# Up projections of three feed-forward blocks by seven half products in place of eight

## The reference

```
# first block, D_FF = 4096
z = rms_norm(h, norm_mlp_g);   h = h + square(relu(z @ w_up)) @ w_down
...                            # gated ple layer, final norm
# second block, D_FF_2 = 2816
def swiglu(x, w_in, w_out):
    gate, up = jnp.split(x @ w_in, 2, axis=-1)
    return (jax.nn.silu(gate) * up) @ w_out
h = h + 0.5 * rms_norm(swiglu(rms_norm(h, ffn1_pre_g), ffn1_w_in, ffn1_w_out), ffn1_post_g)
...                            # mixer: dilated attention and a state-space part (S5)
h = h + 0.5 * rms_norm(swiglu(rms_norm(h, ffn2_pre_g), ffn2_w_in, ffn2_w_out), ffn2_post_g)
```

## Time and profile before

| | |
|---|---|
| time, median of 3 runs | 3018.67 us (3018.64 to 3019.09) |
| span of the profiled execution | 3016.7 us, 2.0 below the median of the runs; no other time of it is given |
| TensorE busy | 2998.1 us, 99% |
| VectorE, ScalarE, GpSimd busy | 1351.8, 870.4, 408.9 us |
| moved by DMA | 206.98 MB, mean 69 GB/s |

### The profile page before, as it was taken

One profiled execution on the slowest core, in us unless ns is written; L12 is line 12 of the kernel. 1 busy time (PEld: TensorE's weight loads), 2 busy tenths in 40 slices (PEclk: granted clock), 3 DMA queues, 4 the chain that ended last, 5 costly groups with the idle time before them and its releaser, 6 DMA issues.

```text
span 3016.7 us, 36793 instructions
## 1 busy us (share of the span) xinstructions
PE 2998.1 (99%) x14144; PEld 2465.9 (82%) x14144; DVE 1351.8 (45%) x1735; ACT 870.4 (29%) x1328; POOL 408.9 (14%) x1004
## 2 busy tenths in 40 slices
PE   8999999999999999999999999999999999999999
PEld 7788888888888888888888888887788888888887
DVE  5854444444445453333333353346655333333335
ACT  6524122112214352111111143136744111111112
POOL 0010000000000001988860010012100000000000
PEclk9999999999999999999999999999999999999999
DMA  3131111111112121222221132212131111111113
GB/s 131 41 108 53 56 56 49 35 56 56 42 42 68 45 85 49 75 97 100 89 82 42 49 133 84 78 63 98 55 133 70 49 49 49 58 54 42 42 49 133
DMA packets 54553, 206.98 MB, mean 69 GB/s; under 512 B 7232, under 2 KB 8000, under 8 KB 52144
## 3 DMA queue, kind: packets, MB, share of 16 engines
q1 hardware_dynamic: 38736, 140.53, 13.9%
q0 software_dynamic: 15712, 65.02, 5.9%
HBM read 173.15 MB, written 31.20 MB: 68 GB/s over the span
## 4 chain that ended last, share of the span: by engine, by line
PE 97%; DVE 2%; ACT 1%; issue 0%; DMA 0%; SPq 0%; DVEq 0%; ACTq 0%
PE ps L128 30%; PE ps L130 30%; PE ps L129 30%; PE ps L1976 1%; PE ps L268 1%; PE ps L1991 1%; PE ps L1950 1%; PE ps L340 0%; PE ps L1626 0%; DVE acc L179 0%; ACT junk L200 0%; PE ps L1659 0%; DVE acc L187 0%; PE ps L1667 0%; ACT junk L166 0%; PE ps L1639 0%
## 5 line engine op out<-in xcount | busy, mean ns | idle before, releaser
L128 PE MATMUL ps<-region_a,region_b 128*128 128x512 f32 x1664 | 654.9, 394 | 1.0 <-DVE region_a L227 1.0
L130 PE MATMUL ps<-region_a,region_b 128*128 128x512 f32 x1664 | 648.0, 389 | 0.0
L129 PE MATMUL ps<-region_a,region_b 128*128 128x512 f32 x1664 | 647.5, 389 | 0.0
L128 PE MATMUL ps<-region_b,region_a 128*128 128x512 f32 x1088 | 428.2, 394 | 0.1
L130 PE MATMUL ps<-region_b,region_a 128*128 128x512 f32 x1088 | 424.9, 391 | 0.0
L947 DVE TENSOR_TENSOR acc<-acc,ps 128x1024 f32<-128x1024 f32 x240 | 292.9, 1220 | 294.0 <-PE ps L130 294.0
L129 PE MATMUL ps<-region_b,region_a 128*128 128x512 f32 x1088 | 424.5, 390 | 0.0
L123 DVE TENSOR_TENSOR region_b<-raw,region_b 128x1024 fp32r<-128x1024 f32 x176 | 216.2, 1244 | 348.5 <-ACT region_b L119 348.2
L128 PEld LDWEIGHTS ps<-region_a,region_b 128*128 128x128 f32 x1664 | 312.5, 188 | 66.4 <-issue 1.8
L130 PEld LDWEIGHTS ps<-region_a,region_b 128*128 128x128 f32 x1664 | 312.4, 188 | 65.2
L129 PEld LDWEIGHTS ps<-region_a,region_b 128*128 128x128 f32 x1664 | 312.6, 188 | 64.3 <-issue 1.7
(11 more groups left out here) (302 smaller groups left out, 3233.6 us busy)
## 6 DMA issues: line engine op xcount, KB each, us to landing
raw<-stream SPq DMA_DIRECT2D x252, 512.0 KB, 3.3
ssm_row<-ssm_mid POOLq DMA_DIRECT2D x8, 1632.0 KB, 7.3
x_mid<-acc POOLq DMA_DIRECT2D x24, 512.0 KB, 3.1
ssm_mid<-made_osc POOLq DMA_DIRECT2D x8, 1024.0 KB, 4.3
ssm_mid<-made_out POOLq DMA_DIRECT2D x8, 608.0 KB, 3.4
acc<-x SPq DMA_DIRECT2D x8, 512.0 KB, 8.1
rold<-x POOLq DMA_DIRECT2D x16, 256.0 KB, 3.7
old_a<-x_mid POOLq DMA_DIRECT2D x8, 512.0 KB, 8.2
```

Source lines behind the costliest of these rows:

```text
L128: nc.tensor.matmul(psum, lhs(0), rhs(0), start=first, stop=False)
L129: nc.tensor.matmul(psum, lhs(0), rhs(1), start=False, stop=False)
L130: return nc.tensor.matmul(psum, lhs(1), rhs(0), start=False, stop=last)
```

## The change

An up pair is now two weight units (256 channels: for `mlp` two hidden blocks, for the gated feeds a gate and an up block). The product of a 2 x 2 arrangement of weight halves (inputs 0 to 511 and 512 to 1023, by column block) with a 2 x 2 arrangement of token pieces (the same input halves, near and far tokens) is formed from seven half products with sums made first (Strassen's scheme in the form with 4 sums of weights and 4 of tokens) and seven joins of results. All up products of a feed come first; the hidden units go to DRAM (`hid`), and are read back for the down products, which run for the near tokens and then for the far ones, each tile summed in PSUM over all hidden units.

The core of the diff:

```diff
-CHUNK = 2
+        SLOTS_UP, AHEAD, AHEAD_DOWN = 7, 6, 3
+        NEAR_K, FAR_K = 2, 4
+        class Quick:
+                order = [(0, 1), (0, 2), (1, 1), (1, 2), (0, 5), (1, 5), (0, 6), (1, 6), (0, 7), (1, 7), (0, 4), (0, 3),
+                         (2, 1), (1, 4), (2, 2), (1, 3)]
+                for p in range(2, pairs):
+                    order += [(p, 6), (p, 7), (p, 4), (p, 5)] + ([(p + 1, 1), (p + 1, 2)] if p + 1 < pairs else []) + [(p, 3)]
...
+            def ring_at(self, i):
+                return (0, 1, 2, 3, 0, 1, 2, 3, 2, 3, 2, 3, 0, 2, 3, 0)[i] if i < 16 else (i + 1) % 4
...
+        def copy_act(act, F, i):
+            p, q = F.order[i]
+            if p >= 2:
+                act.wait_ge(*F.at(f"stored{p % 2}", F.stored_by * (p // 2)))
...
+            act.wait_ge(*F.at("done", i + 1))
+            nc.scalar.activation(F.X(p), ps[:, F.bank_at(i), :], ACT.Copy).then_inc(F.sem["copied"], 1)
...
+        def quick_up_dve(dve, F, hooks={}):
+            for i in range(4, F.N):
+                if i + AHEAD < F.N:
+                    weight_step_dve(dve, F, i + AHEAD)
+                if i > 4:
+                    up_dve_then(dve, F, i - 1)
+                if i not in (6, 7, 8, 9):
+                    up_dve_now(dve, F, i)
+                if i == F.N - 4:
+                    down_lo(dve, F, 0)
+                hooks.get(i, lambda: None)()
...
+        def quick_up_pe(pe, F):
+            N = F.norm
+            for i, (p, q) in enumerate(F.order):
+                pe.wait_ge(*F.at("lo", i + 1))
+                earlier = [j for j in range(i) if F.ring_at(j) == F.ring_at(i)]
+                pe.wait_ge(*(F.emptied(earlier[-1]) if earlier else F.banks_free[i]))
+                for k in range(4):
...
+                    last = products(ps[:, F.bank_at(i), :], lambda h: up_slots[:, i % SLOTS_UP, h, k * P:(k + 1) * P],
+                                    lambda h: F.moving(q, k, h), k == 0, k == 3)
+                    if i == 2 and k == 2:
+                        mixed_turn_pe(pe, F, 0)
+                    if i == 3:
+                        mixed_turn_pe(pe, F, k + 1)
...
+        def quick_stream_sp(sp, F):
...
+            def down(kk):
+                th, k = divmod(kk, F.n)
+                if kk < 2:
+                    sp.wait_ge(*F.raw_read(F.pairs - 2))
+                    sp.wait_ge(*F.at("lo", F.place[F.pairs - 1, 1] + 1))
+                    for cond in F.hid_free:
+                        sp.wait_ge(*cond)
...
+            for p in range(F.pairs):
+                pair(p)
+                if p >= 3:
+                    store(p - 3)
+            down(0)
+            down(1)
+            store(F.pairs - 3)
+            store(F.pairs - 2)
+            store(F.pairs - 1)
+            for kk in range(2, 2 * F.n):
+                down(kk)
...
+        mlp.hid_free = [(res1, 2 * NT)]
+        ffn2.hid_free = [(mix_out, 2 * NT)]
+        ffn1.hid_free = [(s_out, 32 * NB)]
...
-            feed_on_dve(dve, ffn1, mix2_norm_hooks(dve), {(1, 1): lambda: ssm_angle_dve(dve)},
-                        {1: lambda: ssm_growth_dve(dve), 3: lambda: ssm_inverse_dve(dve),
-                         5: lambda: ssm_factors_dve(dve)})
+            weight_lo(dve, ffn1, 2)
+            weight_lo(dve, ffn1, 3)
+            quick_start_dve(dve, ffn1)
+            quick_up_dve(dve, ffn1, {26: lambda: ssm_angle_dve(dve), 40: lambda: ssm_growth_dve(dve),
+                                     46: lambda: ssm_inverse_dve(dve), 52: lambda: ssm_factors_dve(dve)})
+            quick_down_dve(dve, ffn1, behind(ffn1, near_rows_dve(dve, n_mix2)))
+            mix2_tail_dve(dve)
```

More of the change, by code:

```diff
@@ L1051, in first_lo, with ended, down_done, all_stored @@
-        def first_lo(dve, F, us=range(2)):
-            for u in us:
-                make_lo(dve, F.n0 + u, F.W[:, u], (F.n0 + u) % 2)
-        U_MLP = U_OUT + 8
-        mlp = Feed(D_FF1 // P // CHUNK, False, A, B, U_MLP, [(w_out.done, NT)] * 2, True)
-        U_PLE = mlp.last_n
+            def ended(self):
+                return self.at("done", self.N)
+            def down_done(self, kk):
+                return self.at("done", self.N + kk + 1)
+            def all_stored(self, par):
+                return self.at(f"stored{par}", self.stored_by * self.pairs // 2)
@@ new lines, in down_products, with down_part_pe @@
+        def down_products(F, th, kk, i, half, first, last):
+            slot = F.down_slot(kk)
+            return products(ps[:, F.tile_bank(th, i) + half, :], lambda h: slot[:, h, i * P:(i + 1) * P],
+                            lambda h: slot[:, 2 + 2 * h + half, :], first, last)
+        def down_part_pe(pe, F, th, k, i):
+            kk = th * F.n + k
+            pe.wait_ge(*F.at("lo", F.N + 2 * kk + 2))
+            if k == 0 and th == 0 and i >= 2:
+                for r in (2 * (i - 2), 2 * (i - 2) + 1):
+                    pe.wait_ge(*F.emptied([j for j in range(F.N) if F.ring_at(j) == r][-1]))
+            elif k == 0 and th == 1:
+                pe.wait_ge(*F.at("sum", [F.tile_bank(0, x) for x in range(4)].index(F.tile_bank(1, i)) + 1))
+            for half in range(2):
+                last = down_products(F, th, kk, i, half, k == 0, False)
+            return last
@@ new lines, in quick_down_pe @@
+        def quick_down_pe(pe, F, hooks={}):
+            for th in range(2):
+                last_k = NEAR_K if th == 0 else FAR_K
+                for k in range(F.n - last_k):
+                    for i in range(4):
+                        last = down_part_pe(pe, F, th, k, i)
+                    last.then_inc(F.sem["done"], 1)
+                for i in range(4):
+                    for half in range(2):
+                        for k in range(F.n - last_k, F.n):
+                            kk = th * F.n + k
+                            pe.wait_ge(*F.at("lo", F.N + 2 * kk + 2))
+                            last = down_products(F, th, kk, i, half, False, k == F.n - 1)
+                            if i == 3 and half == 1:
+                                last.then_inc(F.sem["done"], 1)
+                        if th == 1 and i == 3 and half == 0 and F.tail:
+                            last.then_inc(F.tail["half"], 1)
+                        if half == 1 and i < 3:
+                            last.then_inc(F.sem["tile"], 1)
+                        if th == 1:
+                            hooks.get((i, half), lambda: None)()
@@ new lines, in tile_done, with tile_sum_dve @@
+        def tile_done(dve, F, t):
+            th, i = divmod(t, 4)
+            if i < 3:
+                dve.wait_ge(*F.at("tile", 3 * th + i + 1))
+            else:
+                dve.wait_ge(*F.down_done((th + 1) * F.n - 1))
+        def tile_sum_dve(dve, F, t):
+            tile_done(dve, F, t)
+            bank = F.tile_bank(*divmod(t, 4))
+            src = ps[:, bank:bank + 2, :].rearrange("p a b -> p (a b)")
+            if F.gated:
+                if t == NT - 1:
+                    dve.wait_ge(*F.all_stored(1))
+                nc.vector.tensor_copy(acc[:, t, :], src).then_inc(F.sem["sum"], 1)
+            else:
+                dve.wait_ge(old_in[t], 16 * F.old_count)
+                nc.vector.tensor_tensor(acc[:, t, :], acc[:, t, :], src, ALU.add).then_inc(F.sem["sum"], 1)
@@ L1251, in qk_unit @@
         def qk_unit(m):
-            free = (ffn1.near_free() if m < 2 else ffn1.at("dn", f1_all)) if m < 4 \
+            free = (ffn1.ended() if m < 2 else f1_down) if m < 4 \
                 else (qk_done, m + 1)
@@ L2344, in last_norm_hooks, with row @@
             N = n_last
-            def behind(t):
+            def row(t):
                 dve.wait_ge(*N.acc_ready(t))
```

1133 lines of the change are left out of this document (652 added, 481 removed).

## The result

The changed kernel takes **3142.23 us** (median of 4 runs, 3141.23 to 3144.8), the kernel before beside it 3018.65: 1.041 of it, 95% interval 1.0396 to 1.0425, so 4.1% slower. The forecast was 3108, the range 3045 to 3150. The direction, and the mechanism that gives it, came out as forecast; the size is 34 us above the point.

A forecast was written before the change was run, and what follows sets the result against it. TensorE's matmuls were taken as the bound, busy 2998.1 of 3016.7 us. First feed -15.8, second +134.3 and third -29.0 gave +89.5, span 3106.2; the median's 2.0 above it made 3108 us, range 3045 to 3150.

The forecast's parts named there:

- third feed: product 12 after the products before: Third feed's start: 7.0 us for late first products, 58.5 to product 12, and 1 of clock.
- second feed: product 12 after T: Second feed's start: 11.3 us late at product 2, 58.5 to product 12, 2 of clock; 71.8 in all.
- second feed: product 150 after T: Second feed's up phase: TensorE finishes product 149 at T + 447 and resumes after the s_out wait, which ends at T + 592.
- The wait that decides: Second feed's down loads: SP waits for GpSimd's state-space stores until T + 592, 145 us after TensorE stopped; feed +131.2.
- the loss per two-input VectorE instruction: GpSimd's state-space work beside VectorE in the second feed: 0.53 us lost per 0.69 us instruction.
- free work: GpSimd's state-space work in the second feed, without store waits and VectorE's hindrance: 303 us.
- Full hold: Rival, second feed: each two-input VectorE instruction holds GpSimd for its full 0.69 us; 3119 us, chance 0.10.
- no slowing: Floor case under the first rival, second feed: GpSimd not slowed by VectorE at all; 3026 us, no separate chance.
- GpSimd takes 367.8 again: First rival, second feed: GpSimd slowed no more than before, wait ends 35 us earlier; 3073 us, chance 0.14.
- VectorE as the bound of every pair: Rival, up phase: VectorE's 20 instructions per pair outlast TensorE's products; 3150 us at 1.0 each, chance 0.05.
- The s_out wait doesn't decide: Rival, second feed: GpSimd is done before product 149, so the kernel gets faster; 2953 us, chance 0.08.
- VectorE's walk: Each feed's start: VectorE's 73 instructions in a row delay products; product 12 starts at 58.5, 22.3 us idle per feed.

The follow-up runs named there:

- hid_moved: Changed kernel with the second feed's hidden rows read from gb's first half and the state-space wait moved to the first norm row; 3014.92 us, 0.9986 against before.
- factors_early: Changed kernel with VectorE's last state-space factors behind product 29 of the second feed, no longer 52; 3094.70 us, -47.5 to the changed kernel.
- extra_dve: Changed kernel with 140 extra two-SBUF-input VectorE subtractions of 512 columns from product 145 of the second feed; 3195.97 us, +53.7 to the changed kernel.
- sums_pool: Changed kernel with GpSimd making the eight weight sums of pairs 0 and 1 at each feed's start, in VectorE's place; 3149.72 us, +7.5.
- joins_first: Changed kernel with VectorE making the weight pieces of products 12 to 16 behind product 10's joins in each feed's start; 3129.85 us, -12.4.
- rows_late: Changed kernel with GpSimd loading the eight old rows behind down unit 5 in the second and third feeds; 3125.07 us, -17.2.
- sp_order: Changed kernel with SP issuing down unit 2's loads ahead of the last pair's store in all three feeds; 3130.21 us, -12.0.

## Why the prediction was right, and where it was 34 us short

The span was forecast at 3106.2 and is 3139.8. By the prediction's own steps (T is the start of the second feed's first product):

| step | forecast | measured | to the sum |
|---|---|---|---|
| start, first feed: product 12 after product 0 | 58.5 + 1 of clock | 64.6 (and 0.2 for product 0) | +5.3 |
| third feed: product 12 after the products before | 7.0 + 58.5 + 1 | 68.7 | +2.2 |
| low clock behind product 12, first and third feed | none | 2.2 and 3.0 | +5.2 |
| second feed: product 12 after T | 71.8 | 74.5 | in the next row |
| second feed: product 150 after T | 599 | 592.5 | -6.5 |
| the last four products | 13.9 | 12.7 | -1.2 |
| first down units (unit 2; in the first feed 4 and 6) | none | gaps 2.5 + 9.5 + 9.1, and 4.4 of low clock | +25.5 |
| a wait of 0.9 near the end of each feed | none | 2.7 | +2.7 |

33.2 of the 33.6 us are found. The waits of 0.9 us stand in every trace behind the change; nothing was run on them.

**The wait that decides** was right in its mechanism and nearly in its size. It is the s_out wait, released by the last store of made_out (shown by hid_moved), and GpSimd behind it (factors_early, extra_dve). T is 1080.2 now. GpSimd started at T + 190.4 (forecast 186.5), TensorE stopped at T + 451.5 (447), the wait ended at T + 583 (592). The mis-sized term is the loss per two-input VectorE instruction: 0.53 read from one pair of rows, 0.44 over whole rounds, 0.39 in extra_dve. It has two effects. Beside VectorE GpSimd is slowed less than I took, and it needed 389.6 us in all where the sum has 402. Against that its free work was taken too small: eight quiet rounds of 35.4, 1.4 for the issues between two of them, and the 24.4 us ahead of them at 0.724 are some 311 us, against 303. With 0.44 in place of 0.53 the sum from the kernel before gives about the same 311. The copy came 2.2 us later behind the wait than my sum says, since its store took 6.7 us to land and not 3.4; four loads were issued just ahead of it, but no run shows that they are the reason. The stall is 141 us where the sum has 152 (447 to 599). That product 150 comes within 6.5 us of its forecast is in part luck, since these errors have different signs.

**The rivals.** Full hold (3119) and no slowing (3026) both fall, with the 0.39 of extra_dve. "GpSimd takes 367.8 again" falls too: it took 389.6. VectorE as the bound of every pair falls with the full steady stretches. "The s_out wait doesn't decide" falls with hid_moved; the 2953 that I gave it weren't reached by hid_moved, since the same work then stands in front of the first norm row. The Trainium skill, "SBUF — State Buffer", section "Who interferes with whom", says that VectorE with two SBUF inputs and GpSimd contend for a shared pair of ports, which is an exclusive lock. The traces agree that each slows the other (extra_dve; sums_pool: 1.5 us for 0.61). Taken as a loss of VectorE's whole 0.69, the rule overstates what these short GpSimd instructions lose (0.39 to 0.44).

**The starts.** VectorE's walk was right up to product 8, which starts 44.0 us after product 0 in the first feed (forecast 43.6). The step past product 10 failed: it had no load in it. I gave product 12 a gap of 2.0 and it has 6.1; joins_first shows it. That the gaps sum to about 21 us per feed, against 22.3, is luck: in front of products 6 and 8 they are 4.3 us shorter than forecast, since slow matmuls fill that time, and in front of product 12 they are 4.1 longer. For the clock I took 1, 2 and 1 us; what it costs behind product 12 was put at nothing.

**The step that failed**, and makes most of the 34 us, is the sentence that the down phase stays full because its loads ask for 145 GB/s of 336. That is a mean over the phase. At its beginning the loads of units 2 and 3, held back by a store in SP's queue, meet 4 MB that GpSimd asks for on the same event, the end of the up phase. With the first feed's 2.5 us, where only the place in SP's queue counts, this cost 25.5 us that the sum put at nothing. rows_late and sp_order show both halves.
